# Two decoder layers on one core: weight loads, state and first projections at the seam between layer 0 and layer 1

## The reference

```
h = rms_norm(x, norm_mix_g) * (1 + sc1) + sh1
z = h @ w_in                       # 11 sections of 1024 columns, 8 heads
A = differential attention, P = causal pooling, R = HGRN2 recurrence, from z
x = x + g1 * ((sig(gA)*A + sig(gP)*P + sig(gR)*R) @ w_out)
h = rms_norm(x, norm_ffn_g) * (1 + sc2) + sh2
q = h @ w_query                    # 8 heads; two halves against 128 keys each
idx, gate = 16 best of the 256 sums of the 16 best of either half
x = x + g2 * sum_k gate_k * gelu(u_tab[idx_k] . h) * v_tab[idx_k]
```

## Time and profile before

| | us |
|---|---|
| median of 3 runs | 2239.7 (2237.44 to 2240.37) |
| span of the profiled execution | 2239.2 (no other time of it is given) |
| PE busy | 1919.8 (86%) |
| DVE busy | 1478.8 (66%) |
| ACT, POOL busy | 674.6, 606.0 |
| mean granted TensorE clock | 0.960 |
| DMA | 713.03 MB, 318 GB/s over the span |
| chain that ended last | PE 49%, DMA 27%, DVE 13%, issue 4% |

### The profile page before, as it was taken

One profiled execution on the slowest core, in us unless ns is written; L12 is line 12 of the kernel. 1 busy time (PEld: TensorE's weight loads), 2 busy tenths in 40 slices (PEclk: granted clock), 3 DMA queues, 4 the chain that ended last, 5 costly groups with the idle time before them and its releaser, 6 DMA issues.

```text
span 2239.2 us, 22101 instructions
## 1 busy us (share of the span) xinstructions
PE 1919.8 (86%) x6452; PEld 1121.6 (50%) x6452; DVE 1478.8 (66%) x4012; ACT 674.6 (30%) x1867; POOL 606.0 (27%) x588
## 2 busy tenths in 40 slices
PE   4999999978878878887779999998889788779776
PEld 3677777644434433433257777775434334334332
DVE  5676676676766766767545676666776666666774
ACT  1222232233333333333212232231333333333332
POOL 3000000044444444444200000002444444444342
PEclk9999999989999999999889999999999999999989
DMA  9555445189999999999964345423999999999995
GB/s 380 199 232 205 167 178 204 45 361 421 421 421 421 421 421 422 419 418 421 407 229 158 148 151 205 194 85 152 382 421 421 422 421 421 421 421 420 420 412 245
DMA packets 116344, 713.03 MB, mean 318 GB/s; under 512 B 12816, under 2 KB 17168, under 8 KB 48656
## 3 DMA queue, kind: packets, MB, share of 16 engines
q0 software_dynamic: 73728, 536.90, 57.9%
q1 hardware_dynamic: 42512, 174.97, 20.8%
HBM read 710.78 MB, written 1.05 MB: 318 GB/s over the span
## 4 chain that ended last, share of the span: by engine, by line
PE 49%; DMA 27%; DVE 13%; issue 4%; POOL 2%; ACT 2%; SPq 2%; another core or an unknown queue 0%; DVEq 0%; POOLq 0%; ACTq 0%
DMA wall<-in_peer_uv,idx 25%; PE PS L994 13%; PE PS L756 10%; PE PS L761 9%; DVE wall L1035 5%; PE PS L766 5%; PE PS L968 3%; PE PS L801 2%; POOL wall L530 2%; DMA braw<-in_ada_rows 1%; PE PS L776 1%; SPq L368 1%; ACT M L691 1%; DVE pos L1474 1%; PE PS L742 1%
## 5 line engine op out<-in xcount | busy, mean ns | idle before, releaser
L994 PE MATMUL PS<-wall,M 128*128 128x512 f32 x2048 | 979.5, 629 | 240.2 <-ACT M L691 240.2
L1035 DVE CUSTOM_DVE_ANT_0 wall<-wall,tok 128x1024 f32<-128x1024 f32 x512 | 604.4, 1223 | 398.1 <-DMA wall<-in_peer_uv,idx 398.0
L994 PEld LDWEIGHTS PS<-wall,M 128*128 128x128 f32 x2048 | 395.6, 200 | 788.5 <-issue 429.1
L530 POOL DMA_INDIRECT wall<-in_peer_uv,idx x512 | 560.9, 1095 | 763.3 <-PE PS L994 353.6
L677 ACT ACTIVATE dg<-dg 128x2 f32<-128x2 f32 x256 | 52.0, 203 | 799.3 <-DVE dg L1035 799.3
L756 PE MATMUL PS<-hT,wall 128*128 128x256 f32 x1120 | 247.8, 380 | 0.0
L487 POOL TENSOR_SCALAR rsb<-ms 128x4 f32<-128x4 f32 (+2 forms) x23 | 5.5, 238 | 839.0 <-DVE ms L1035 838.8
L756 PEld LDWEIGHTS PS<-hT,wall 128*128 128x128 f32 x1120 | 211.7, 190 | 29.9
L761 PE MATMUL PS<-wall,hT 128*128 128x512 f32 x512 | 225.5, 594 | 0.0
L691 ACT ACTIVATE M<-ident,wgt 128x128 f32<-128x128 f32 x512 | 177.5, 394 | 24.3 <-ACT wgt L684 0.7
L761 PEld LDWEIGHTS PS<-wall,hT 128*128 128x128 f32 x512 | 96.6, 191 | 109.4 <-issue 108.6
(11 more groups left out here) (237 smaller groups left out, 1726.2 us busy)
## 6 DMA issues: line engine op xcount, KB each, us to landing
wall<-in_w_in SPq DMA_DIRECT2D x128, 704.0 KB, 11.0
braw<-in_ada_rows SPq DMA_DIRECT2D x80, 512.0 KB, 4.3
ring<-in_peer_w_query SPq DMA_DIRECT2D x14, 1024.0 KB
wall<-in_w_out SPq DMA_DIRECT2D x2, 4096.0 KB, 15.5
wall<-in_peer_uv,idx POOLq DMA_INDIRECT x512
wall<-in_ada_rows SPq DMA_DIRECT2D x6, 1024.0 KB, 12.3
pwt<-in_pool_w SPq DMA_DIRECT2D x8, 256.0 KB, 2.7
wall<-in_peer_w_query SPq DMA_DIRECT2D x2, 1024.0 KB, 4.8
```

Of the source, the lines that this page charges most:

```text
L530: nc.gpsimd.indirect_dma_start(out=pair_rows[b][s], out_offset=None, in_=uv_rows, in_offset=bass.IndirectOffsetOnAxis(ap=idx[i % 2][:, k:k ...
L994: ins = mm(bank(B_ACC + 2 * t + hf), diag[:, b, s, :], pair_rows[b][s][:, D + hf * 512:D + (hf + 1) * 512], start=(i == FIRST_TILE[t] and ...
L1035: return v.tensor_tensor_reduce(out=o, in0=a, in1=b, scale=1.0, scalar=0.0, op0=ALU.mult, op1=ALU.add, accum_out=acc)
```

## The change

SP, before layer 1's weights: it first waits until the last gather (group 127) has landed, then loads all eight pieces of head 0, early block 0 and the pool weights, then the eight of head 1, then the early blocks 1 to 3. The waits for freed places stay.

The first 128 tokens' state of layer 1 is made inside layer 0's last groups: the squares of group 116 (LEAD) signal POOL, which makes the root ahead of its gather 123; DVE folds the columns of `adac` and scales this tile in its turn 123; PE makes its eight transposes after the expert sum of group 125, and ACT copies them out after weighing group 126.

In layer 1, POOL and DVE treat the second tile alone, and the first three units of head 0 are made in two halves of 128 tokens (`project_halves`). Ahead of pieces 6 and 7 of the first half stand the second tile's eight transposes. DVE takes one early block ahead of the forget gates and three behind.

```diff
@@ -73,6 +73,8 @@
...
+B_LEAD = (B_S0, B_S1)
+B_REST = (B_LA, B_LB)
...
@@ -89,6 +91,7 @@
...
+LEAD = (LAST_TILE[0] + 1) * GROUPS + 4
...
@@ -402,14 +407,22 @@
...
+                    load_pool(0)
+                    load_early_blocks(range(EARLY_BLOCKS[l]))
                 else:
 
-                    for g in range(LGROUPS - NBUF, LGROUPS):
-                        sp.wait_ge(s_vacc, summed(l - 1) + g + 1)
-                        for j in range(2):
-                            load_w(j, j, [k for k in range(KC) if freed_by(j, k) == g], j == 0)
-                load_pool(0)
-                load_early_blocks()
+                    last = LGROUPS - 1
+                    sp.wait_ge(s_uv[last % NBUF], 16 * GROUP * buffer_uses(l - 1, last))
+                    for j in range(2):
+                        for g in range(LGROUPS - NBUF, LGROUPS):
+                            chunks = [k for k in range(KC) if freed_by(j, k) == g]
+                            if chunks:
+                                sp.wait_ge(s_vacc, summed(l - 1) + g + 1)
+                                load_w(j, j, chunks, j == 0)
+                        if j == 0:
+                            load_early_blocks(range(1))
+                            load_pool(0)
+                    load_early_blocks(range(1, EARLY_BLOCKS[l]))
                 load_blocks(0)
 
                 def load_pair(g, last):
@@ -499,7 +516,7 @@
...
             for l in range(DEPTH):
                 if l:
-                    rsqrt(NR * l, NT, D)
+                    rsqrt(NR * l, 1, D, 1)
...
@@ -514,6 +531,9 @@
...
+                    if g == LEAD + NBUF + 1 and l + 1 < DEPTH:
+                        pool.wait_ge(s_lead_ms, l + 1)
+                        root(1, D, 0).then_inc(s_lead_rs, 1)
...
@@ -545,14 +565,31 @@
...
+            def lead_evac(l):
+
...
-                        i = nc.scalar.activation(hT[:, k, :], bank(B_S0 + b)[:, (k % 2) * T:(k % 2 + 1) * T], ACT.Identity,
+                for half in range(2):
+                    act.wait_ge(s_tp, NTP * l + half + 1)
+                    for k in range(4 * half, 4 * half + 4):
+                        i = nc.scalar.activation(hT[:, k, 0:P], bank(B_LEAD[half])[:, k % 4 * P:(k % 4 + 1) * P], ACT.Identity,
                                                  bias=adac[:, l, k:k + 1], scale=adac[:, l, KC + k:KC + k + 1])
                     i.then_inc(s_hTa, 1)
+
...
+                    for k in range(4):
+                        i = nc.scalar.activation(hT[:, k, P:T], bank(B_REST[0])[:, k * P:(k + 1) * P], ACT.Identity,
+                                                 bias=adac[:, l, k:k + 1], scale=adac[:, l, KC + k:KC + k + 1])
+                    i.then_inc(s_hT_rest, 1)
                 if l == 0:
                     act.wait_ge(s_pcol, 1)
...
@@ -705,6 +742,8 @@
...
+                    if g == LEAD + 9 and l + 1 < DEPTH:
+                        lead_evac(l + 1)
...
@@ -723,14 +762,46 @@
...
+
+                def turn_rest():
+
+                    pe.wait_ge(s_tok, NTOK * l + 1)
+                    for half in range(2):
+                        for k in range(4 * half, 4 * half + 4):
+                            i = nc.tensor.transpose(bank(B_REST[half])[:, k % 4 * P:(k % 4 + 1) * P],
+                                                    tok[:, 1, k * P:(k + 1) * P], ident[:])
+                        i.then_inc(s_tp, 1)
+
+                def project_halves():
+
+                    pe.wait_ge(s_qev, HEADS * l)
+                    pe.wait_ge(s_scfree, len(TILES) * l)
+                    for t in range(NT):
+                        for k in range(KC):
+                            if t == 0 and k == KC - 2:
+                                turn_rest()
+                            if t == 0 and k % 4 == 0:
+                                pe.wait_ge(s_hTa, NHTA * l + k // 4 + 1)
+                            elif k == 0:
+                                pe.wait_ge(s_hT_rest, l)
+                            elif k == 4:
+                                pe.wait_ge(s_hTd, l + 2)
+                            if t == 0:
+                                pe.wait_ge(s_wc[k], 16 * (l + 1))
+                            for u in range(3):
+                                for i, s in enumerate(((AQ, AK), (HQ, HF), (PP,))[u]):
+                                    o = i * T + t * P
+                                    ins = mm(bank(B_Z[u])[:, o:o + P], wz[0][:, k, s, :], hT[:, k, t * P:(t + 1) * P],
+                                             start=(t == 0 and k == 0 and i == 0), stop=(k == KC - 1), skip_group_check=True)
+                                if t == NT - 1 and k == KC - 1:
+                                    ins.then_inc(s_z, 1)
 
                 def project_first():
 
-                    if l:
-                        pe.wait_ge(s_zev, H0 * UNITS)
...
@@ -1015,6 +1089,13 @@
...
+                    if g == LEAD + 9 and l + 1 < DEPTH:
+                        pe.wait_ge(s_lead_tok, l + 1)
+                        for half in range(2):
+                            for k in range(4 * half, 4 * half + 4):
+                                ins = nc.tensor.transpose(bank(B_LEAD[half])[:, k % 4 * P:(k % 4 + 1) * P],
+                                                          tok[:, 0, k * P:(k + 1) * P], ident[:])
+                            ins.then_inc(s_tp, 1)
...
@@ -1152,15 +1234,22 @@
...
-                if l:
+                if l == 0:
+                    fold_cols(adac[:, l, :], l, 0, NFIRST).then_inc(s_a1, 1)
+                    dve.wait_ge(s_a1, l + 1)
+                    evac_hT(l)
+                    constants()
+                else:
                     mean_squares((1,))
-                fold_cols(adac[:, l, :], l, 0, NFIRST).then_inc(s_a1, 1)
-                if l:
-                    scaled(NR * l)
-                dve.wait_ge(s_a1, l + 1)
-                evac_hT(l)
-                if l == 0:
-                    constants()
+                    dve.wait_ge(s_rs, NR * l + 1)
+                    scale_rows(1).then_inc(s_tok, 1)
+                    dve.wait_ge(s_tp, NTP * l + 4)
+                    for k in range(4, KC):
+                        i = sts(hT[:, k, P:T], bank(B_REST[1])[:, k % 4 * P:(k % 4 + 1) * P], adac[:, l, KC + k:KC + k + 1],
+                                adac[:, l, k:k + 1], ALU.mult, ALU.add)
...
@@ -1437,10 +1526,11 @@
...
                 n_early = EARLY_BLOCKS[l]
-                for i in range(n_early // 2):
+                n_ahead = (n_early // 2, 1)[l]
+                for i in range(n_ahead):
                     early_dots(i)
                 forget(0, 0)
-                for i in range(n_early // 2, n_early):
...
@@ -1616,10 +1706,18 @@
...
-                    if g == (LAST_TILE[0] + 1) * GROUPS + 4:
+                    if g == LEAD:
                         ch(add_experts(0))
                         ch.sync()
-                        ch(dot(tok[:, 0, :], xs[:, 0, :], xs[:, 0, :], ms[:, 0:1]))
+                        i0 = dot(tok[:, 0, :], xs[:, 0, :], xs[:, 0, :], ms[:, 0:1])
+                        if l + 1 < DEPTH:
+                            i0.then_inc(s_lead_ms, 1)
+                        else:
+                            ch(i0)
+                    if g == LEAD + 7 and l + 1 < DEPTH:
+                        fold_cols(adac[:, l + 1, :], l + 1, 0, NFIRST).then_inc(s_a1, 1)
+                        dve.wait_ge(s_lead_rs, l + 1)
+                        scale_rows(0).then_inc(s_lead_tok, 1)
...
```

More of the change, by code:

```diff
@@ L376, in load_pool, with load_early_blocks @@
                                  pool_scale[l:l + 1, bass.ds(g * T, T)].to_broadcast([P, T])).then_inc(s_pw, 16)
-                def load_early_blocks():
-                    for i in range(EARLY_BLOCKS[l]):
+                def load_early_blocks(blocks):
+                    for i in blocks:
                         b = BLOCK0[l] + i
@@ L481, in _, with root @@
             last.then_inc(s_const, 1)
-            def rsqrt(k, n, width, c=0):
-                pool.wait_ge(s_ms, k + 1)
+            def root(n, width, c):
                 apart(pool)
@@ L488, in rsqrt @@
                 pc.sync()
-                nc.gpsimd.tensor_tensor(rs[:, c:c + n], rsb[:, c:c + n], mhalf[:, 0:n], ALU.pow).then_inc(s_rs, 1)
+                return nc.gpsimd.tensor_tensor(rs[:, c:c + n], rsb[:, c:c + n], mhalf[:, 0:n], ALU.pow)
+            def rsqrt(k, n, width, c=0):
+                pool.wait_ge(s_ms, k + 1)
+                root(n, width, c).then_inc(s_rs, 1)
             rsqrt(0, NT, D)
@@ L546, in evac_hT @@
                                      ACT.Copy).then_inc(s_hTa, 1)
-            for l in range(DEPTH):
+            def lead_evac(l):
                 act.wait_ge(s_a1, l + 1)
-                for b in range(2):
-                    act.wait_ge(s_tp, NTP * l + b + 1)
-                    for k in (2 * b, 2 * b + 1):
```

(43 more changed lines are left out.)

17 lines of the change are left out of this document (12 added, 5 removed).

## The result

| | before | after |
|---|---|---|
| median, us | 2239.89 (2237.44 to 2240.37, 4 runs) | 2225.53 (2223.54 to 2228.52, 4 runs) |
| ratio | | 0.9933, 95% interval 0.9921 to 0.9945 |
| span of the profiled execution | 2239.2 | 2221.8 (its time was 2223.54) |
| mean granted TensorE clock | 0.960 | 0.967 |
| PE busy | 1919.8 | 1911.5 |

A forecast was written before the change was run, and what follows sets the result against it. Bound: the wait chain at the layer seam, 1097 to 1164 us, with a 29.47 us landing and projections waiting for all the state. Seam 17.9 us shorter, less 0.6, is 17.3; 2239.7 - 17.3 = 2222.4 us, range 2218 to 2231.

The forecast's parts named there:

- The landing: End of layer 0: without weights beside it, the last gather lands 20.0 us after issue in place of 29.47.
- Rival F: Last gathers of layer 0: gathers themselves are slow, landing no earlier; gain only 8.5 us, 2231; chance 0.04.
- The weights behind it: After the last landing: head 0's eight pieces take 16.1 us, to 1133.3; upper bound 18.1.
- The state: Layer seam: second 128 tokens' state scaled at 1130.6, 3.8 us before PE reaches its transposes.
- Products: Head 0's first units, layer 1: 80 narrow products at 0.224 us replace 40 at 0.432, 0.6 us more over all.
- rival D: Head 0's narrow products: bound by their weight loads, adding 8.6 us, 2231.0; chance 0.04.
- Rival B: First half of head 0's projections: PE's clock stays low between pieces; gain 10.8 us, 2228.9; chance 0.14.
- Rival E: Past the projections: lower clock lasts on to head 0's scores, slower than before, 2265.5 us; chance 0.04.
- Work laid into layer 0's last groups: First tile's root, folds, scaling, transposes and copies: cost taken as 0, bounds 2 us on POOL, 0.4 on ACT.
- The early blocks behind the forget gates: DVE, layer 1: blocks 1 to 3 done by 1170.5, before head 0's scores at 1175.1; covered by 4.6 us.
- Rival C: DVE's early blocks behind the forget gates: run without overlap, head 0's softmax 9.9 us late, 2232.3; chance 0.10.
- The sum: Layer seam: projections end at 1146.5 for 1164.4, 17.9 us earlier; less 0.6 allowance, a gain of 17.3.

The follow-up runs named there:

- e3: Changed kernel with SP's old order, pieces loaded as groups free their places and no wait for the last landing: 2230.63 us, ratio 0.9961 to the kernel before.
- e7: Changed kernel with only head 1's pieces waiting for the last landing, head 0's issued among the gathers: 2233.91 us beside 2241.2 for the kernel before.
- e2: Kernel before with only SP's wait and new load order and DVE's shift of one early block: 2229.22 us, ratio 0.9955 to the kernel before.
- e5: Changed kernel with three unused dots on DVE ahead of the second tile's mean square: 2226.0 us beside 2241.2 for the kernel before.
- e6: Changed kernel with eight unused dots on DVE ahead of the second tile's mean square: 2236.35 us beside 2241.2 for the kernel before.
- e4: Changed kernel with head 0's first three units made at full 256-column width after both tiles' state: 2231.38 us, ratio 0.9965 to the kernel before.
- e8: Changed kernel with SP waiting for the landing of group 126 in place of 127: 2221.56 us beside 2241.2 for the kernel before.
- e1: Changed kernel run again, unedited: median 2224.25 us over 6 runs, ratio 0.9934 to the kernel before.
- e11: Kernel before profiled again, unedited: one run at 2239.47 us.

## Why the prediction was right, point by point

**The landing.** 20.0 us after the issue forecast, 20.00 measured, by the row of the end of layer 1. Spacing 4.98 forecast, 4.93 measured. e3 and e7 show the cause: with SP's transfers beside the gathers the landing is 29.4, and e2 shows that the wait alone brings it to 19.98. Rival F is out.

**The weights behind it.** 16.1 us forecast for eight pieces, 16.8 measured (1117.90 to 1134.70). It was mis-sized by 0.7: I had 13.8 at the full rate and 2.3 beside it, and those 2.3 are 3.0. A part stands at the start, where the share is 0.43 in 1118:1120. Besides, the queue moved 6.30 MB up to the last piece's landing where the eight are 5.77, so transfers issued behind them had begun to share the rate. The upper bound of 18.1, with early blocks among the pieces, was not reached.

**The state.** 1130.6 forecast; 1131.26 measured in a run whose seam starts 0.8 later, so 33.3 us after the issue against 33.5. e5 and e6 put it on the right side of the weights.

**Products.** 0.224 forecast for a narrow one; 94 passes in 10.51 us are 0.112 each, 0.224 the pair. A wide one is 0.432. So halving the width costs 4% here, and rival D is out. The rule that I weighed against the change, in the Trainium skill, TensorE: Matmul & The Clock Gate, section Back-to-back issue gap, by which a 128-column matmul in a stream would keep about three quarters of the price of a 256-column one, does not hold for these float32 products. (My estimate by it, 17.5 us and 2227.6, should have read 17.7 and 2227.8; that changes nothing in the argument.)

**The clock.** Rival B asked that bursts of 1.35 us with gaps for a DMA run at the half clock. They did not: granted clock 1.00 from 1124 to 1148, with gaps of 0.24 to 1.04. What did lose the clock were stands of 5.78 (e4) and 5.14 us (e6), the 3.65 of the earlier trace rows, and one of 2.10 in e8, at the start of the sum behind it. The section HAM oscillation of the same page describes the bad case; with gaps as short as these, this case does not show it. Rival E needed a low clock and is out with B.

**Work laid into layer 0's last groups.** Forecast at nothing. From the issue of gather 121 to the issue of the last one it is 25.59 us before and 25.61 to 25.68 in the kernels with the early state: at most 0.1. ACT's eight copies take 2.89 (3.0 forecast) and are done at 1119.73; ACT is then idle 0.63 us before it weighs group 127.

**The early blocks behind the forget gates.** Covered, by more than I worked out (4.6). In the timeline of the changed kernel:

```profile
1155.22 1.23 DVE L1116 CUSTOM_DVE_ANT_0 braw<-braw,crow 128x1024 f32<-128x1024 f32 x1 [2.63 <-DMA braw<-in_ada_rows]
...
1177.16 1.14 DVE L1113 SCALAR_TENSOR_TENSOR ssc<-nd,slopes,PS 128x384 f32<-128x384 f32 x2 [8.94 <-PE PS L858]
```

DVE is idle 8.94 us before head 0's scores. Rival C is out. The scores come at 1177.16 for 1192.98, 15.8 earlier in runs whose seams start 0.8 apart, so 16.6 of the seam's 16.9 arrive there.

**The sum.** Forecast: 17.3 us of seam. Measured: 67.26 - 50.39 = 16.87, and the two spans differ by 17.4 (the seam starts 0.8 later, the rest is 1.3 shorter). From the issue of the last gather to unit 3 I had worked out 49.37 and allowed 0.6 on top; it was 50.39. The 1.02 between are: the landing -0.07, the weights +0.68, from the last piece's landing to the end of PE's products +0.27 (13.47 for 13.2), and the wait for ACT +0.14. So the allowance of 0.6, put down for passes at the lower clock or a late piece, about covers the late pieces; no pass ran at the lower clock, and the other 0.4 were not in the sum. The copies of unit 0 I had not looked at: with wide products unit 0 is complete three products of 0.432 before the end, 1.3 us, and the two copies (0.66 together) fit; with narrow ones it is 0.67, and they just don't. One slip in the range: with the state as the end, 21.7 less gives 2218.0, not 2218.2.

**The medians.** They differ by 14.4 and, in e1, by 15.0, not by 16.9, and the changed kernel's median is 3.1 us over the forecast. Three things are seen. The changed kernel's time was 1.7 us over its span, as in e1 and e11 (1.7 and 1.8), so that the profiled execution of before was likely some 1.0 over its median. The profiled execution of the changed kernel was the fastest of its four, 2.0 under its median; 14.4, 1.0 and 2.0 are the 17.4 between the spans. And a second profile of before had a seam of 66.00; with that one the gain is 15.6. So the forecast of the seam was worked out from one long execution of before and then taken off the median; that it fits the one profile to 0.4 us is in part luck. The interval of 12.3 to 17.7 holds all of them. How far the rest of the spread comes from the seam or from other stages stays open.

## What to carry to other kernels

Prefetching beside the last transfers of a stage is not free when the stage's end is itself a landing: here 6.2 to 6.6 MB moved beside the last gathers put 9.4 us on the last one, and weights issued behind it cost less, without half-width work for PE to do on the pieces as they came (seams of 67.26 or 66.00 and, in e2, 55.54) and with it (58.42 and 50.39). Before you move work off the critical path, ask what PE stands on meanwhile: the early state at full width gained nothing (e4), since PE still stood 5.78 us and then paid in clock. Consume pieces in the order in which they land (3.0 us here).

## What the runs showed of the hardware that I had not expected

**The last landing is a thin tail.** For 6 us before the last gather lands, the 16 DMA engines are busy at 0.10 and then 0.04 (33 and 16 GB/s), about one of them at a time: in 1112:1116 the gathers' queue moves 15 packets, mostly of 8 KB, one after the other. The end of layer 1 in the kernel before, where nothing follows, has the same tail (0.08, 0.06 and 0.03 in 2214:2220, ahead of a landing at 2219.51), so the change did not make it. Weights issued 5.8 us before the landing delay it by 0.9 us (e8); SP's transfers among the last gathers, issued from 1103.42 on (e7), delay it by 9.4. By the landing they had moved 6.60 MB, 15.8 us at 419 GB/s; that they delay it by 6.4 less fits with the empty tail taking the rest, which is arithmetic and not a run of its own. A wait for the landing therefore leaves the queue nearly empty for 6 us, and for part of 2 more until the new transfers flow (share 0.43 in 1118:1120). I had read the last stretch as a full queue.

**Small gaps and the clock.** A stand of 2.10 us was followed by an expert sum of 5.40 us in e8, one of 1.22 by 3.70 in the changed kernel. But in e3 and e7 stands of 2.23 and 2.21 were followed by 3.70, and a stand of 3.65 by 6.52 in the kernel before and by 5.40 in e11. So the length of the last stand alone does not tell what the next sum costs, and these runs do not show what does.
